# The experts' products of a decoder step: tokens stationary, weights moving 512 columns wide, in split float32r passes

## The reference, cut to what matters

```python
def _swiglu(h, w_gate, w_up, w_down):
    return (jax.nn.silu(h @ w_gate) * (h @ w_up)) @ w_down

def _moe_swiglu(h, w_r, b_r, e_gate, e_up, e_down):
    logits = (h @ w_r).astype(jnp.float32) + b_r.astype(jnp.float32)
    top_v, top_i = lax.top_k(logits, TOP_K)                 # 2 of 8
    wts = jax.nn.softmax(top_v, axis=-1)
    gate = jnp.sum(jax.nn.one_hot(top_i, N_EXPERTS) * wts[..., None], axis=-2)
    out = jnp.zeros_like(h)
    for e in range(N_EXPERTS):
        out = out + gate[..., e:e + 1] * _swiglu(h, e_gate[e], e_up[e], e_down[e])
    return out
```

## Time and profile before

| what | value |
|---|---|
| time, median of 3 runs (lowest to highest) | 1968.59 us (1967.38 to 1971.02) |
| the profiled execution: span of its instructions | 1965.7 us; it has no time of its own beside the span |
| busy: PE, PEld, DVE, ACT, POOL | 83%, 74%, 39%, 22%, 14% of the span |
| expert stage, first gather to last scatter | from 1355 to 1938 us of the span |
| HBM read, mean rate | 312.97 MB, 161 GB/s over the span |

### The profile page before, as it was taken

How to read it: one execution, slowest core, us unless ns; L and a number is a source line. 1 busy time by engine, 2 the same in 40 slices (tenths; PEclk the granted TensorE clock), 3 DMA queues, 4 the chain that set the end, 5 groups by cost and what they waited for, 6 DMA issues and landing times.

```text
span 1965.7 us, 31838 instructions
## 1 busy us (share of the span) xinstructions
PE 1634.8 (83%) x12493; PEld 1458.5 (74%) x12493; DVE 764.2 (39%) x1378; ACT 436.1 (22%) x612; POOL 282.5 (14%) x148
## 2 busy tenths in 40 slices
PE   3894589597887876999894995886999999999994
PEld 1893344396876844999794994874999999999993
DVE  3446633534534533111005546413333423433343
ACT  2012222221111102433222112211213213222321
POOL 2002023000000001565552003330000000000000
PEclk8997788786876787999897996796999999999997
DMA  8345689302022031444333432130766676786772
GB/s 308 129 149 207 269 307 378 131 1 86 0 86 87 0 134 62 134 144 139 145 123 122 149 114 72 47 104 22 267 214 248 243 270 230 242 287 220 257 255 91
DMA packets 51834, 318.17 MB, mean 162 GB/s; under 512 B 6384, under 2 KB 6528, under 8 KB 19712
## 3 DMA queue, kind: packets, MB, share of 16 engines
q1 hardware_dynamic: 44640, 289.91, 41.2%
q0 software_dynamic: 7136, 27.47, 4.0%
HBM read 312.97 MB, written 4.39 MB: 161 GB/s over the span
## 4 chain that ended last, share of the span: by engine, by line
PE 61%; issue 17%; DVE 10%; POOL 4%; ACT 3%; DMA 2%; DVEq 2%; ACTq 0%; SPq 0%; POOLq 0%
PE ps L316 19%; PE ps L1964 16%; PE ps L1276 7%; PE ps L1938 4%; POOL wsplit L295 4%; PE ps L1947 2%; PE ps L336 2%; PE ps L384 1%; PE ps L609 1%; DVE hT L425 1%; PE ps L1266 1%; DVE arena L1716 1%; PE ps L1704 1%; DVE hT L405 1%; PE ps L800 1%
## 5 line engine op out<-in xcount | busy, mean ns | idle before, releaser
L316 PE MATMUL ps<-hx_hi,wsplit 128*128 128x320 f32 x1376 | 310.5, 313 | 62.8 <-DVE hx_lo L441 54.2
L1964 PE MATMUL ps<-arena,ring 128*128 128x128 f32 x2816 | 323.1, 276 | 6.2 <-ACTq L2030 4.9
L1964 PEld LDWEIGHTS ps<-arena,ring 128*128 128x128 f32 x2816 | 320.0, 193 | 10.9 <-ACT arena L2028 6.2
L316 PEld LDWEIGHTS ps<-hx_hi,wsplit 128*128 128x128 f32 x1376 | 234.5, 191 | 66.9 <-issue 64.9
L295 POOL TENSOR_TENSOR wsplit<-ring,wsplit 128x2048 fp32r<-128x2048 f32 (+1 forms) x42 | 209.2, 4985 | 260.6 <-ACT wsplit L305 260.6
L316 PE MATMUL ps<-hx_lo,wsplit 128*128 128x320 f32 x688 | 214.7, 312 | 0.0
L1276 PE MATMUL ps<-arena 128*128 128x128 f32 (+1 forms) x960 | 141.4, 323 | 9.6 <-ACT arena L1233 8.9
L1276 PEld LDWEIGHTS ps<-arena 128*128 128x128 f32 (+1 forms) x960 | 136.9, 233 | 14.9 <-ACT arena L1233 10.5
L2059 DVE TENSOR_TENSOR arena<-arena,ps 128x128 f32<-128x128 f32 x88 | 25.2, 287 | 292.3 <-ACT arena L2015 292.3
L316 PEld LDWEIGHTS ps<-hx_lo,wsplit 128*128 128x128 f32 x688 | 131.2, 191 | 0.0
L316 PE MATMUL ps<-wexp,he_hi 128*128 128x256 f32 x704 | 127.8, 284 | 0.0
(11 more groups left out here) (331 smaller groups left out, 2367.7 us busy)
## 6 DMA issues: line engine op xcount, KB each, us to landing
ring<-in_exp_gu SPq DMA_DIRECT2D x91, 1024.0 KB, 4.9
ring<-in_w_mod SPq DMA_DIRECT2D x48, 1024.0 KB, 8.2
ring<-in_exp_down SPq DMA_DIRECT2D x32, 1408.0 KB, 7.7
ring<-in_ffn_gu SPq DMA_DIRECT2D x22, 1024.0 KB, 4.9
arena<-in_cache_v POOLq DMA_DIRECT2D x64, 256.0 KB, 5.6
arena<-in_cache_k SPq DMA_DIRECT2D x64, 256.0 KB, 5.4
ring<-in_w_in_o SPq DMA_DIRECT2D x16, 1024.0 KB, 4.9
ring<-in_w_in_e SPq DMA_DIRECT2D x13, 1024.0 KB, 4.9
```

What stands on the lines that cost most here:

```text
L316: mm = nc.tensor.matmul(out, u, v, start=first and p == 0, stop=last and p == 2)
L1964: mm = nc.tensor.matmul(ps[:, j % 2, gu * CAP:gu * CAP + CAP], w[:, gu * KT + q, :], xg[:, q, :], start=q == 0, stop=q == KT - 1)
```

## The change

Gate and up turn around: the gathered tokens, split into `xg_hi` and `xg_lo`, are stationary, and the weights move, 512 columns at a time (256 gate and 256 up columns of the same hidden units; the last piece has 128 and 128), in three float32r passes. So every gate/up and down weight is now split. The weights lie in HBM in 17 chunks per expert (11 gate/up, 6 down, of which the last is half as large) of 2048 floats per partition, and go through five slots of the same memory (`ESLOT`): slots 0 to 3 take turns, slot 4 holds chunk 4 alone. ACT makes hi of chunk j + 4 when PE has finished chunk j; lo is made by DVE, or by POOL for chunks 2, 5, 8, 11 and 14. SP loads a chunk when lo of the chunk before it in its slot is done.

The hidden values come out with tokens on the partitions, so PE transposes them (`turn_hidden`, 11 more transposes), and ACT and DVE split them from PSUM. The gate weight is no longer in the scatter matrix: three more one-column products in the gather bring it to the slots (`gslot`), and the hidden values are multiplied with it. The scatter is then a product with the 0/1 matrix itself, in two float32r passes (`ye_hi`, `ye_lo`), and the gather's third block has 128 rows, padded with zeros. Down moves 512 columns. `acc` lies where `hT` lay, and POOL clears the buffers. The first four chunks are split before the router's copies on ACT, and in the router's code on DVE and on POOL.

The core of the diff, lines shortened, with the new order of each engine (the old loop bodies, which are removed, are in the code above):

```diff
+UNITS = 6
+ESLOT = [0, 1, 2, 3, 4] + [0, 1, 2, 3] * 3
+AHEAD, EARLY = 4, 5
+UNIT_END = {1: 0, 3: 1, 5: 2, 7: 3, 9: 4, 10: 5}
+TURNED_AT = {3: 0, 5: 1, 7: 2, 9: 3, 10: 4, 11: 5}
+LO_OF_POOL = [j for j in range(N_EXP) if j % 3 == 2]
+LO_OF_DVE = [j for j in range(N_EXP) if j % 3 != 2]
...
+    def expert_hi(act, j, t):
+        wait_landed(act, j, t)
+        act_copy(expert_part(j, 0), expert_raw(j)).then_inc(e_hi, 1)
+    def expert_lo(eng, subtract, j, t):
+        eng.wait_ge(e_hi, t * N_EXP + (j + 1))
+        subtract(expert_part(j, 1), expert_raw(j), expert_part(j, 0).bitcast(F32), ALU.subtract
+                 ).then_inc(e_lo_pool if j in LO_OF_POOL else e_lo_dve, 1)
...
     def expert_tensor(pe):
+            for u in range(UNITS):
+                pe.wait_ge(e_hid, t * UNITS + (u - 1 + HID0))
+                for j in [j for j in range(N_EGU) if min(j // 2, UNITS - 1) == u]:
+                    wait_lo(pe, j, t)
...
+                        mm = three_passes(ps[:, u % 2, 0:n], (xg_hi[:, q, :], xg_lo[:, q, :]),
+                                          [v[:, k, :] for v in w], q == 0, q == KT - 1)
+                if u == 0:
+                    pe.wait_ge(ex_ye, t + 1)
+                    scatter_tensor(pe, 0, ex_sc.sem)
+                if u == 1:
+                    pe.wait_ge(ex_acc.sem, ex_acc.at("A", t))
+                    scatter_tensor(pe, 1, ex_sc.sem)
+                if u:
+                    turn_hidden(pe, u - 1, t)
...
+                if u == 3:
+                    pe.wait_ge(ex_select, t + 2)
+                    pe.wait_ge(ex_psel_in, t + 2)
+                    pe.wait_ge(ex_acc.sem, ex_acc.at("B", t))
+                    gather_tensor(pe)
+            for c in range(N_EDN):
+                wait_lo(pe, j, t)
+                pe.wait_ge(e_het, t * UNITS + (c + 1 + HID0))
...
     def expert_scalar(act):
+            for j in range(N_EXP):
+                act.wait_ge(e_done, t * N_EXP + (j + 1))
+                if j in UNIT_END:
+                    nc.scalar.activation(sgE[u % 2][:, 0:n], ps[:, u % 2, 0:n], ACT.Silu)
+                if j == N_EXP - 1:
+                    act_copy(ye_hi, ps[:, 4:6, :])
+                if j + AHEAD < N_EXP:
+                    expert_hi(act, j + AHEAD, t)
+                else:
+                    expert_hi(act, j + AHEAD - N_EXP, t + 1)
+                if j in TURNED_AT:
+                    act.wait_ge(e_turned, t * UNITS + (u + 1))
+                    act_copy(he_hi[:, tiles, :], src)
+                if j == 5:
+                    act_copy(PselT[:, :], ps[:, 3, 0:T])
+                if j == N_EGU - 1:
+                    tokens_hi(act)
...
     def expert_vector(dve):
+            for j in range(N_EXP):
+                if j in UNIT_END:
+                    nc.vector.scalar_tensor_tensor(hE, sgE, gslot, ps[:, u % 2, n:2 * n], ALU.mult, ALU.mult)
+                if j == N_EXP - 1:
+                    nc.vector.tensor_tensor(ye_lo, ps[:, 4:6, :], ye_hi, ALU.subtract)
+                if (j + AHEAD) % N_EXP in LO_OF_DVE:
+                    expert_lo(dve, nc.vector.tensor_tensor, (j + AHEAD) % N_EXP, t)
+                if j in TURNED_AT:
+                    nc.vector.tensor_tensor(he_lo[:, tiles, :], src, he_hi[:, tiles, :], ALU.subtract)
+                if j in (2, 4):
+                    dve.wait_ge(ex_sc.sem, ex_sc.at("A" if j == 2 else "B", t))
+                    accumulate_vector(j // 2 - 1).then_inc(ex_acc.sem, 1)
+                if j == 6:
+                    dve.wait_ge(ex_psel_t, t + 1)
+                    select_vector(dve, e + 1)
+                if j == N_EGU - 1:
+                    tokens_lo(dve)
+        each_expert(dve, body, after_round)
+        dve.drain().then_inc(last_ye, 1)
...
+    def expert_pool(pool):
+        for j in LO_OF_POOL:
+            if j < AHEAD:
+                expert_lo(pool, nc.gpsimd.tensor_tensor, j, 0)
+        nc.gpsimd.memset(h2tok[:, 2, :], 0.0).then_inc(ye_zero, 1)
+        nc.gpsimd.memset(PselT[:, :].bitcast(F32), 0.0).then_inc(ex_psel_in, 1)
+        nc.gpsimd.memset(ye_hi[:, :].bitcast(F32), 0.0).then_inc(ye_zero, 1)
+        nc.gpsimd.memset(ye_lo[:, :].bitcast(F32), 0.0).then_inc(ex_ye, 1)
+        pool.wait_ge(rt_pe.sem, rt_pe.at("rank"))
+        nc.gpsimd.memset(acc[:, :, :], 0.0).then_inc(ye_zero, 1)
...
         norm_scalar(act, 3)
+        expert_early_scalar(act)
         router_scalar(act)
```

More of the change, by code:

```diff
@@ L1747, in program @@
     h2tok = aE.take(3, D)
[L1748 to L1753, removed]
-    Psel = aE.take(3, CAP)
[L1755 to L1761, removed]
+    acc = hT
+    sgE = [aE.take(256) for _ in range(2)]
+    hE = [aE.take(256) for _ in range(2)]
+    Psel = aE.take(3, CAP)
+    gcol = aE.take(3)
+    gslot = aE.take(1)
+    aRt = Area((NES * 2 - 1) * ESIZE)
+    lgT = aRt.take(T)
+    lg = aRt.take(3, NE)
+    ex = aRt.take(3, NE)
+    cmpA = aRt.take(3, 64)
+    cmpB = aRt.take(3, 64)
+    beaten = aRt.take(3, NE)
     sel = aE.take(3, NE + 1)
@@ L1829, in router_vector @@
         nc.vector.memset(lg[:, :, :], 0.0)
-        nc.vector.memset(acc[:, :, :], 0.0)
+        for j in LO_OF_DVE:
+            if j < AHEAD:
+                expert_lo(dve, nc.vector.tensor_tensor, j, 0)
         dve.drain()
@@ L1898, in each_expert @@
                 after_round()
[L1900 to L1917, removed]
@@ L1919, in expert_raw, with same_slot @@
-    def expert_raw(j):
[L1920 to L1932, removed]
+    def same_slot(j, t):
+        back = [q for q in range(j) if ESLOT[q] == ESLOT[j]]
+        if back:
+            return back[-1], t
+        return max(q for q in range(N_EXP) if ESLOT[q] == ESLOT[j]), t - 1
@@ new lines, in expert_raw, with expert_size, expert_part, expert_weights @@
+    def expert_raw(j):
+        flat = ring[:, :, :].rearrange("p s n -> p (s n)")
+        return flat[:, ESLOT[j] * ESIZE:ESLOT[j] * ESIZE + expert_size(j)]
+    def expert_size(j):
+        return ESIZE // 2 if j == N_EXP - 1 else ESIZE
+    def expert_part(j, which):
+        return wexp[:, 2 * ESLOT[j] + which, 0:expert_size(j)]
+    def expert_weights(j):
+        n = 2 * P if j == N_EGU - 1 else 4 * P if j < N_EGU else D
+        return [expert_part(j, x).rearrange("p (k n) -> p k n", n=n) for x in range(2)]
@@ L1936, in gather_tensor @@
             for n in range(3):
[L1937 to L1941, removed]
+                nc.tensor.matmul(ps[:, 6 + q // 4, (q % 4) * CAP:(q % 4) * CAP + CAP],
+                                 h2tok[:, n, q * P:q * P + P], Psel[:, n, :],
+                                 start=n == 0, stop=n == 2)
+        for n in range(3):
+            mm = nc.tensor.matmul(ps[:, 3, 3 * P:3 * P + 1], Psel[:, n, :], gcol[:, n:n + 1],
+                                  start=n == 0, stop=n == 2)
+        mm.then_inc(ex_gather, 1)
     def scatter_tensor(pe, hf, done):
@@ L2037, in select_vector @@
                                     sel[:, n, ds(e, 1)], ALU.is_equal, ALU.mult)
-        dve.drain()
-        for n in range(3):
-            last = nc.vector.tensor_scalar(Pgat[:, n, :], Psel[:, n, :], gate[:, n, ds(e, 1)],
-                                           None, ALU.mult)
-        last.then_inc(ex_dve.sem, 1)
+        nc.vector.tensor_copy(gcol.unsqueeze(2), gate[:, :, ds(e, 1)]).then_inc(ex_select, 1)
     def accumulate_vector(hf):
@@ L2074, in body @@
                     select_vector(dve, e + 1)
-            for j in range(2, N_ED):
-                down_lo(dve, j, t)
+                if j == N_EGU - 1:
+                    dve.wait_ge(ex_xg_hi, t + 2)
+                    tokens_lo(dve)
         def after_round():
```

283 lines of the change are left out of this document (167 added, 116 removed).

## The result

The changed kernel takes 2035.32 us (median of 4 executions, 2027.77 to 2040.99), the kernel before 1969.57 beside it (1967.38 to 1971.02). The ratio is 1.0328 with an interval of 1.031 to 1.0347. The forecast was 2017, with a range of 1950 to 2036.

The account below looks back on a forecast made before the run. PE was taken to bound the kernel. Eight experts +38, entry +3.8 and exit +7.0 gave +48.8 on the 1965.7 us span: 2014; with the timed median 2.9 above the span, 2017 us, range 1950 to 2036.

Parts of the forecast that it names:

- The tail of the turn is covered: End of an expert: hi and lo of c11 to c16 each end at least 3 us before PE wants them.
- PE's own work: PE's products, passes and transposes in one expert after the change: 55.4 us (54.5 to 61.3), 14.1 shorter without waits.
- Wait ahead of scatter B: PE idles 6.0 us per expert for accumulate A, behind lo(6) in DVE's order; 3.0 without exclusion.
- Wait ahead of the gather: PE idles 7.5 us per expert for select, behind lo(10), if POOL is let in; 3.1 if not.
- the first rival: DVE keeps the lock shared with POOL through select: 67.4 us an expert, 1963 us; chance 0.22.
- the second (no exclusion): DVE and POOL don't exclude each other, or DVE is early enough: 61 us an expert, 1905 us; chance 0.12.
- The wait for he_lo(1): PE's transposes ahead of the gather wait 0.4 us for this small op; 0.5 in the expert's sum.
- The clock: PE's clock falls to half after the 6.0 and 7.5 us waits, costing 2.4 us each; none after 3.1.
- Entry: Norm 3 to first gather: held tensor_scalars +4.6, memsets +1, gather -3.0, lo of gathered tokens +1.2; together +3.8 us.
- Exit: The last scatter waits for DVE's whole loop body, a ninth expert's lo(3) included: +7.0 us.
- more is lost: Rival: 3.05 us per clock fall, 0.243 per wide pass, landings late by 0.5; 2055 us at most; chance 0.08.
- the gather doesn't gain: Rival: the gather doesn't gain from full rows, +2.9 us an expert, +23 within any case; no chance given.

Follow-up runs that it names:

- the last kernel: All lo parts on DVE, with accumulate (one chunk earlier still), select and he_lo ahead of lo, against the kernel before: 1866.80 us, ratio 0.9466.
- the run without POOL: The changed kernel with all 17 lo parts made by DVE, its order as changed, POOL keeping only memsets: 1962.69 us, ratio 0.9953.
- The run with PE's filler: The changed kernel plus 24 unread passes of 320 columns on PE ahead of its wait for accumulate A: 2027.07 us, ratio 1.028.
- the ordered kernel with all lo on DVE: The changed kernel with accumulate, select and he_lo ahead of lo in DVE's order, and all lo parts on DVE: 1879.32 us, ratio 0.9528.

## Why the prediction was right, and where it was off

The forecast was slower by 2.4%, by the two waits and the clock; it was 3.3%, by those and one more. The two long waits and the price of an expert without waits stand as shown by the runs above; the step that failed is "The tail of the turn is covered". That the time still lies in the range is luck in part: it is 0.7 us inside the upper end and beyond 2034, the end of the terms themselves, since no term stood for the third wait.

- *PE's own work*, 55.4: the last kernel's period without its wait is 56.18 - 0.34 = 55.8. The terms written out add up to 55.5. In the changed kernel's timeline of PE every third wide pass starts 0.68 us later, 0.227 each, the value taken:

```profile
1599.94 0.39 PE L310 MATMUL ps<-wexp,he_lo 128*128 128x512 f32 x1
...
1600.62 0.39 PE L310 MATMUL ps<-wexp,he_lo 128*128 128x512 f32 x1
```

- *Wait ahead of scatter B*, 6.0: measured 6.25, by the links named (POOL's lo(5), DVE's lo(6), accumulate A). One link came late: hi(5) was ready 10.2 us after the last chunk, not 9.1, behind two loads of ACT's function table that the working leaves out. DVE's lo(4) ended only then too (1614.48), so this did not show. Of the two ends that were kept, 3.0 without exclusion and 6.0 with it, the run without POOL gave 3.97 for the first: there DVE makes lo(5) too.
- *Wait ahead of the gather*, 7.5: measured 6.80. POOL was let in between lo(10) and select in every one of the eight experts, so the step called the weakest held, and the first rival (DVE keeps the lock) fell, as did the second (no exclusion).
- *The wait for he_lo(1)*, 0.5: measured 0.55.
- *The turn's tail*, nothing: this is the step that failed, 2.0 us an expert, 16 over the eight. I compared hi and lo of c11 to c16 with the time at which PE wants them, and these are early enough. But PE transposes hidden values ahead of c11, and that waits for he_lo(3), a small op that stands behind lo(13) in DVE's order. DVE's timeline:

```profile
1663.03 2.29 DVE L1951 TENSOR_TENSOR wexp<-ring,wexp 128x2048 fp32r<-128x2048 f32 x1 [0.39 <-ACT wexp L299]
1665.23 0.42 DVE L2146 TENSOR_TENSOR he_lo<-ps,he_hi 128x256 fp32r<-128x256 f32 x1
```

  lo(13) itself is early; what it delays is not. PE goes on at 1665.80. The run with he_lo ahead of lo took this wait away, and with it and its like 13.8 us.
- *The clock*, 2.4 after each long wait: 75.9 - 55.8 - 15.6 = 4.5 for both. The run with PE's filler gives 2.15 for the first, and the gathers' mean of 7.8 (62.5/8) against 5.62 gives 2.2 for the second. That no fall follows a wait near 3 us, on which the prices of the first two rivals rest, was wrong: without POOL's parts it fell after 3.97 and after 2.62 in every expert.
- *Expert*: 55.4 + 6.0 + 2.4 + 0.5 + 7.5 + 2.4 = 74.2 against 75.9; the differences are +0.4, +0.25, +0.05, -0.7, +2.0 and -0.3.
- *Entry*, +3.8: measured +0.7, with two terms off that go against each other. The norm was held for longer than 5.6: its four tensor_scalars (1.38 in the earlier trace rows) took 8.59, through POOL's lo(2) and through all four memsets, which kept their turn (timelines of POOL and of DVE):

```profile
1332.29 4.51 POOL L1951 TENSOR_TENSOR wexp<-ring,wexp 128x2048 fp32r<-128x2048 f32 x1 [14.82 <-ACT wexp L299]
1336.73 0.95 POOL L2185 MEMSET arena<- 128x1024 f32 x1
...
1338.82 0.95 POOL L2188 MEMSET ye_lo<- 128x1024 f32 x1
```

```profile
1331.96 8.59 DVE L419 TENSOR_SCALAR hT<-hT,gsc,modT 128x256 f32<-128x256 f32 x4
```

  That is 7.2 us more. The first gather, costed at 12.1 as if all of it were at half clock, took 7.8 with its one-column products (15.07 in the earlier trace rows), since the clock came back inside it (0.76 on average). With 64 rows in place of full ones, in the runs above, the first gather stayed at half clock to its end and took 15.06.
- *Exit*, +7.0: measured +6.3. The terms put there, 7.6 + 0.5 - 0.65, make 7.4. The last scatter waits 7.9 for the end of DVE's loop where it waited 0.95 before, and 0.7 of that came back behind it.
- *Transfers*, nothing: in the expert stage a DMA ends 0.2 us of waiting in all, one of ACT's, although a landing takes 6.1 us where the earlier trace rows has 4.9.
- *The last two rivals*: "more is lost" fell in each of its terms (2.15 and 2.2 a fall, 0.227 a pass, 0.2 us of waiting for transfers in all), "the gather doesn't gain" by the runs with 64 rows.

The sum 48.8 became 64.3: +16.1 in the experts, -3.1 at the entry, -0.7 at the exit, and +3.3 from the start of norm 3, which no term stood for. Of the 16.1, some 13 are the 1.7 an expert above, the third wait less what the other terms gave back; the rest lies in the first and the last turn, which are not like the six between. The timed median stands 5.3 above the profiled span, where 2.9 was taken.

## What to carry to other kernels

Before work is put on engines that have slack on average, write down each engine's order at every place where the bounding engine waits for it, small ops included, and ask which op stands ahead of the one that is wanted: here three blocks moved ahead of another in one engine's order turned 3.3% slower into 3.6% faster. Two engines that shut each other out work like one, and here the slower one's share was a loss: the same order with all lo parts on the faster engine was 20 us faster. A wait costs more than its length where the clock falls after it: the waits ahead of scatter B, 49.4 us in all, were worth 65.5 us of time.

## What was not expected of the hardware

- POOL's memsets, which only write SBUF, held DVE's tensor_scalars: 0.95 us for 1024 elements a partition, and in the changed kernel DVE stood still through all four. In the kernels without POOL's splits the two took turns, 2.93 us for four tensor_scalars instead of 1.38, and tensor_tensors with two SBUF operands beside the last memset took 0.41 and 0.43 as always. What decides who goes first stays open. Timeline of DVE, all lo parts on DVE, order as changed:

```profile
1333.07 2.93 DVE L419 TENSOR_SCALAR hT<-hT,gsc,modT 128x256 f32<-128x256 f32 x4
1335.93 0.41 DVE L423 TENSOR_TENSOR hT<-hT,gsc 128x256 f32<-128x256 f32 x1
```

- At full clock 64-row products made the gather dearer than full rows: 48 products with 16 of them at 64 rows took 8.52 us, with all at 128 rows 5.62. The profile before had shown 8.26 at full clock, but not which products were to blame.
- ACT loads its function table twice in every expert of the changed kernel, ahead of SiLU and ahead of the copies; the kernel before did so once (8 loads in its expert stage). In the chain of the ordered kernel with all lo on DVE both loads, 1.28 us each, stand ahead of the hi part behind which its wait of 1.76 us ends. The groups by shape, changed kernel, expert stage:

```profile
L299 ACT ACT_TABLE_LOAD x8 | 10.3, 1283 | 6.3 <-PE ps L310 6.2
L2077 ACT ACT_TABLE_LOAD x8 | 10.3, 1283 | 0.1
```

- With PE's filler the clock fell after 2.8 us of idle time in five experts and held in two, with the same work on PE before it. After 2.0 us ahead of the last turns it held in seven of eight experts of the changed kernel and fell in seven of eight with accumulate and select ahead. What decides between them stays open.
